# One denominator chain for both scan directions, another bank pair for the second context update, and a reordered first output tile and end, in a diffusion block

## Chip, cores and metric

The kernel runs on one core of one Trainium2 chip. The metric is device time in microseconds (us), lower is better. The engines are PE (TensorE, the matrix products), DVE (VectorE), ACT (ScalarE), POOL (GpSimd) and SP (SyncE, which issues most transfers). Each runs its own instructions in order and waits for the others on semaphores.

## What is computed

One layer of a hybrid backbone on 1024 latent and 256 context tokens of 1024 channels, in float32: a normalisation, a token mixer with two branches (a bidirectional chunkwise mLSTM and a gated MLP), an output projection, a SwiGLU feed-forward and a final normalisation. The change lies in the mLSTM scan, in the output projection and at the final normalisation. The scan, cut to what matters (one direction of one head, chunks of 128 tokens):

```python
def step(carry, inp):
    C, n, m = carry
    ...
    num = s @ v + w_prev[..., None] * (q @ C)
    den = sum(s, axis=-1) + w_prev * (q @ n)
    h = num / max(abs(den), exp(-m_t))[..., None]
    kw = k * w_src[..., None]
    C_new = w_c * C + kw.T @ v
    n_new = w_c * n + sum(kw)
...
out = merged @ w_out
...
xs = xs + g2x * swiglu(...)
return rmsnorm(xs, final_g)
```

## The kernel before

All float32 products of the projections are done in three products of a reduced format: an operand x is split into x_hi (ACT copies it) and x_lo (DVE subtracts), and hi·hi, hi·lo and lo·hi are summed. A stage of weights is one 1 MB block in two halves `raw[0]`, `raw[1]`, split into `whi`, `wlo`; SP loads the next block into a half as soon as DVE has signalled `w_ready` for it.

**The heads.** Four heads run one after the other (head 0 written out, heads 1 and 2 in a loop of PE, head 3 written out), in `head` on PE and `attend` on DVE. After the head's projections the scan runs over ten steps j of one chunk each, two of them context (j = 0, 1), in both directions d at once. In step j PE makes, for each direction, the update product `kw·vaug` (L2274, signal `dc_done`), into bank 2 + d of PM (PSUM has eight banks: PD[0], PD[1] with two each, PM with four). DVE reads the bank and makes the next state from it, `Cst` (L1593, L1597, signal `c_ready`); the next update may overwrite the bank after that. From j = 2 on PE also makes the numerators and the denominator of the latent chunk in one bank: the chunk's own part `work·vaug` (L2291) and the part of the past `WB·Cst` (L2292, signal `num_done`). DVE makes from the denominator's column a small chain of three instructions on 128x1 (`den`, L1611, L1613, L1614), each waiting for the one before (`own.link`), and then scales the 256 numerators into `Hh` (L1617, or L1620 in the second half, signal `h_written`). One 128x256 piece of the `wlo` split of the next head's weights (L1365) is done in each of the steps 2 to 9. On DVE a step therefore stands as: two state updates, one split piece, then chain and scaling of direction 0, then of direction 1. `work` is made ahead of the scan from the scores in banks 0 and 1 of PM (L1583, signal `sw_ready`).

After the scan PE goes on with the next head's projection (`channels`, L2095; in head 3 `v_part`, L2218), which needs the split weights' second half from its fifth of eight k on, while DVE normalises `Hh`; then PE transposes `Hh` (L2307), and DVE multiplies by the output gate (L1632).

**The output projection.** `out_tile(hf, t)` (L2422) makes one tile of 128 tokens x 512 columns: 8 k x 3 products. A tile of 512 columns uses two weight blocks of 256, buffers A and B. Tiles 0 to 3 of the first half are made for k = 0 to 6, then for k = 7; tile 4 waits until DVE has added tile 0 to the residual (`residual`, L1854 and L1857, signal `out_res`). ACT splits block B (L894) only when PE has made the last product of the stage before; DVE follows (L1357).

**The end.** The last stage makes token tiles 0 to 7 of the feed-forward's output (L2527). DVE adds each to the residual (L2018; tile 7 in halves, L2055), ACT sums the squares (L1330, L1333), DVE makes 1/sqrt of the mean by a chain of 12 instructions (`rsqrt`, L1344 to L1350), scales the tile by it and by the gain (`write_out`, L2043), and SP stores it (L697, L701). Tile t - 1 is finished behind the sum of tile t. Tile 6 is finished ahead of and between the sums of the two halves of tile 7.

Of the kernel before, what the change touches and what calls it, by code (L numbers as in the profile page):

```python
# [29 lines left out]
F32 = mybir.dt.float32  # L30
F32R = mybir.dt.float32r
I32 = mybir.dt.int32
ALU = mybir.AluOpType
# [4 lines left out]
P = 128  # L38
D = 1024
# [27 lines left out]
LINKS_H = 74  # L67
# [55 lines left out]
def build(nc, x, c, ctx, c_ctx, w_ada, b_ada, norm1_g, norm2_g, w_in, conv_w, conv_b, gate_b, head_g,  # L123
# [17 lines left out]
    with es:  # L141
# [25 lines left out]
        with ExitStack() as sM:  # L167
# [24 lines left out]
            with ExitStack() as sH:  # L192
# [9 lines left out]
                with ExitStack() as s1:  # L202
# [6 lines left out]
                    den = sb("den", [P, 2, 4], stack=s1)  # L209
# [74 lines left out]
        with ExitStack() as sF:  # L284
# [21 lines left out]
            with ExitStack() as s7:  # L306
                fg = sb("fg", [P, D], stack=s7)
                junkF = sb("junkF", [P, D], stack=s7)
            sa = sb("sa", [P, 2, NLAT], stack=sF)
# [18 lines left out]
        PD = [es.enter_context(nc.psum_tensor(f"PD{s}", [P, 2 * HALF], F32)) for s in range(2)]  # L328
# [58 lines left out]


# [494 lines left out]
        def _(act):  # L883
# [108 lines left out]
            def o_out(h, T, m):  # L992
# [3 lines left out]
                nc.scalar.activation(sgo[:, m, :], PD[m][:, :], ACT.Tanh, scale=0.5).then_inc(slot_free[m], 1)  # L996
                act.wait_ge(slot_free[m], h * 5 + 6)
# [35 lines left out]
            o_out(0, T_H, 0)  # L1033
            weights_b(0)
            weights_d(0)
            o_out(0, T_H, 1)
            split_hi(96, A)
            squares(0)
# [3 lines left out]
            with act.Fori(1, HEADS) as h:  # L1042
# [14 lines left out]
                for m in range(2):  # L1057
                    o_out(h, T, m)
                split_hi(h * 64 + 96, A)
                own.enter(h, LT, 1)  # L1060
# [276 lines left out]
        def _(dve):  # L1337
# [31 lines left out]


# [196 lines left out]
            def attend(h):  # L1567
# [17 lines left out]
                for j in range(TT):  # L1585
                    for d in range(2):
# [3 lines left out]
                        bank = PM[:, (2 + d) * HALF:(2 + d) * HALF + DVA - 1]  # L1590
# [9 lines left out]
                    if j >= 2:  # L1600
                        split_lo_piece(h * 3 + (N_H + 3), A, j - 2)
                    if j < CT:
                        continue
                    for d in range(2):

                        t = tile_of(d, j)
                        at = d * HALF if j % 2 else 0
                        bank = (PM if j % 2 else PD[d])[:, at:at + DV]
                        bden = (PM if j % 2 else PD[d])[:, at + DV:at + DV + 1]
                        dve.wait_ge(num_done, h * 16 + (2 * (j - CT) + d + 1))  # L1610
                        own.link(v.tensor_scalar(den[:, d, 0:1], bden, -1.0, hc[:, 2, d, t:t + 1],  # L1611
                                                 ALU.mult, ALU.max))
                        own.link(v.tensor_tensor(den[:, d, 1:2], bden, den[:, d, 0:1], ALU.max))  # L1613
                        own.link(v.reciprocal(den[:, d, 2:3], den[:, d, 1:2]))  # L1614
# [438 lines left out]
            for e in range(2):  # L2053
# [3 lines left out]
                if e == 0:  # L2057
                    write_out(LT - 2, whole)
# [528 lines left out]
```

## Time and profile before

| | |
|---|---|
| median of 3 runs | 1810.24 us (1808.37 to 1811.42) |
| profiled execution | 1810.4 us |
| its span, first to last instruction | 1808.7 us |
| PE busy | 1760.9 us (97%) |
| DVE, ACT, POOL busy | 1081.5, 602.0, 168.8 us |
| granted TensorE clock, mean | 0.993 of full speed |

The profiled execution took 1.7 us more than its span. "Busy" sums the time in which an engine had an instruction under way; products overlap, so 97% doesn't say that PE could not be faster. Times below are counted from the span's start. L12 is line 12 of the kernel before.

### The profile page before, as it was taken

What the parts mean: (1) busy time and instruction counts of PE and PEld (TensorE: products, weight loads), DVE (VectorE), ACT (ScalarE), POOL (GpSimd) and SP (SyncE); (2) the same over time, 40 slices, a digit from 0 to 9 for tenths busy, and PEclk for the clock granted to TensorE, in tenths of its full rate; (3) what the DMA queues carried; (4) which work ended last, traced back from release to release, by engine and by line L of the source; (5) the groups of instructions that cost most, each with busy time, mean ns of one, the idle gap of its engine ahead of it and who ended that gap; (6) DMA issues with size and microseconds to landing.
All of it is one profiled execution on the core that took longest, in us unless ns stands there. A gap on an engine that the chain in (4) does not pass through costs nothing.

```text
span 1808.7 us, 23195 instructions
## 1 busy us (share of the span) xinstructions
PE 1760.9 (97%) x8556; PEld 1469.8 (81%) x8556; DVE 1081.5 (60%) x1706; ACT 602.0 (33%) x937; POOL 168.8 (9%) x212
## 2 busy tenths in 40 slices
PE   6899999999999999999999999999999999999997
PEld 3697887979788888888888788888888888888886
DVE  4677636575457767546333436865655656566657
ACT  6533241422233324445210213443443333221112
POOL 1002020200212001111100100000000001222210
PEclk9999999999999999999999999999999999999999
DMA  7211110212059123433533343122222232722212
GB/s 305 70 49 35 59 47 24 78 38 71 12 179 319 51 82 100 154 119 132 217 95 98 124 149 128 36 98 89 70 93 70 85 101 70 276 108 93 95 44 94
DMA packets 100131, 187.76 MB, mean 104 GB/s; under 512 B 5810, under 2 KB 74562, under 8 KB 95714
## 3 DMA queue, kind: packets, MB, share of 16 engines
q1 hardware_dynamic: 83906, 130.11, 21.0%
q0 software_dynamic: 16160, 56.77, 8.9%
q8 instruction: 42, 0.69, 0.2%
q14 instruction: 23, 0.19, 0.0%
HBM read 150.11 MB, written 36.75 MB: 103 GB/s over the span
## 4 chain that ended last, share of the span: by engine, by line
PE 89%; DVE 7%; issue 2%; ACT 1%; DMA 0%; DVEq 0%; SPq 0%; ACTq 0%
PE PD L2095 23%; PE PM L2507 11%; PE PD L2507 11%; PE PD L2527 7%; PE PM L2527 6%; PE PD L2422 5%; PE PD L2381 4%; PE PM L2381 4%; PE PD L2205 4%; PE PD L2111 4%; PE PD L2218 1%; PE PM L2441 1%; PE PD L2441 1%; PE PM L2358 1%; PE PD L2180 1%
## 5 line engine op out<-in xcount | busy, mean ns | idle before, releaser
L2095 PE MATMUL PD<-R_hi,whi 128*128 128x512 f32 x480 | 149.3, 392 | 0.0
L2095 PE MATMUL PD<-R_lo,whi 128*128 128x512 f32 x480 | 148.0, 390 | 0.0
L2095 PE MATMUL PD<-R_hi,wlo 128*128 128x512 f32 x480 | 147.8, 389 | 0.0
L867 POOL TENSOR_TENSOR w_raw<-w_raw,g2B 128x2048 f32<-128x2048 f32 x11 | 50.8, 4620 | 652.4 <-DMA w_raw<-in_w_ff 488.4
L2095 PEld LDWEIGHTS PD<-R_lo,whi 128*128 128x128 f32 x480 | 90.1, 188 | 19.0
L2095 PEld LDWEIGHTS PD<-R_hi,wlo 128*128 128x128 f32 x480 | 90.1, 188 | 19.0
L2095 PEld LDWEIGHTS PD<-R_hi,whi 128*128 128x128 f32 x480 | 89.0, 188 | 18.3 <-issue 0.5
L1888 DVE TENSOR_TENSOR ws_lo<-S,ws_hi 128x512 fp32r<-128x512 f32 x76 | 56.3, 742 | 77.2 <-ACT ws_hi L1239 77.2
L894 ACT ACTIVATE whi<-raw 128x1024 fp32r<-128x1024 f32 x56 | 56.2, 1049 | 127.1 <-PE PD L2095 124.5
L2111 PE MATMUL PD<-whi,R_hi 128*128 128x256 f32 x256 | 72.7, 284 | 0.8 <-ACT vaug L960 0.8
L2111 PE MATMUL PD<-wlo,R_hi 128*128 128x256 f32 x256 | 72.4, 283 | 0.0
L2111 PE MATMUL PD<-whi,R_lo 128*128 128x256 f32 x256 | 72.4, 283 | 0.0
L2018 DVE TENSOR_TENSOR xs<-PM,xs 128x1024 f32<-128x1024 f32 x39 | 47.6, 1222 | 34.6 <-PE PM L2527 34.6
L2018 DVE TENSOR_TENSOR xs<-PD,xs 128x1024 f32<-128x1024 f32 x40 | 48.2, 1221 | 32.5 <-PE PD L2527 32.5
L1357 DVE TENSOR_TENSOR wlo<-raw,whi 128x1024 fp32r<-128x1024 f32 x48 | 56.6, 1219 | 6.8 <-ACT whi L894 6.8
L1239 ACT ACTIVATE ws_hi<-S 128x512 fp32r<-128x512 f32 x76 | 47.5, 625 | 31.8 <-DVE S L1902 17.4
L1239 ACT ACTIVATE ws_hi<-rawF 128x512 fp32r<-128x512 f32 x60 | 37.6, 629 | 57.8 <-PE PD L2507 30.4
L2527 PE MATMUL PM<-R_lo 128*128 128x512 f32 x240 | 56.5, 389 | 0.0
L2527 PE MATMUL PD<-R_lo 128*128 128x512 f32 x240 | 56.2, 389 | 0.0
L2527 PEld LDWEIGHTS PD<-R_lo 128*128 128x128 f32 x240 | 45.0, 188 | 9.4
L2527 PEld LDWEIGHTS PM<-R_lo 128*128 128x128 f32 x240 | 45.0, 188 | 9.3
L2527 PE MATMUL PD<-R_hi,f_hi 128*128 128x512 f32 x192 | 51.4, 390 | 0.6 <-issue 0.6
(486 smaller groups left out, 4632.3 us busy)
## 6 DMA issues: line engine op xcount, KB each, us to landing
rawF<-in_w_ff SPq DMA_DIRECT2D x44, 512.0 KB, 4.8
ada<-in_w_ada POOLq DMA_DIRECT2D x32, 512.0 KB, 5.7
raw<-in_w_in SPq DMA_DIRECT2D x30, 512.0 KB, 5.3
f_dram<-Fo SPq DMA_DIRECT2D x11, 1024.0 KB, 4.8
w_raw<-in_w_ff SPq DMA_DIRECT2D x11, 1024.0 KB, 4.9
f_raw<-f_dram SPq DMA_DIRECT2D x11, 1024.0 KB, 6.8
ada_raw<-in_w_ada SPq DMA_DIRECT2D x8, 1024.0 KB, 18.9
rawG<-in_w_in SPq DMA_DIRECT2D x16, 512.0 KB, 4.9
```

The lines of the kernel that those rows point to most:

```text
L894: nc.scalar.activation(whi[buf][:, half * 4 * CW:(half + 1) * 4 * CW], raw[half][:, :], ACT.Copy).then_inc(hi_done, 1)
L1239: nc.scalar.activation(ws_hi[n][:, :, :], left_source(buf, n, sums), ACT.Copy).then_inc(left_hi_d, 1)
L1357: v.tensor_tensor(wlo[buf][:, at], raw[half][:, :], whi[buf][:, at].bitcast(F32), ALU.subtract).then_inc(w_ready[half], 1)
L1888: v.tensor_tensor(ws_lo[n][:, :, :], source, ws_hi[n][:, :, :].bitcast(F32), ALU.subtract)\
L2018: v.tensor_tensor(xs2[:, t, :], wide[t % 4], xs2[:, t, :], ALU.add).then_inc(summed, 1)
L2095: i = mm(dst[:, e * HALF:e * HALF + width], wk[:, k, :], part, start=(k == 0 and step == 0), stop=(k == KT - 1 and step == 2))
L2111: i = mm(PD[s][:, e * HALF:e * HALF + CW], src[:, k, at], wk[:, k, :], start=(k == 0 and step == 0), stop=(k == KT - 1 and step == 2))
L2205: last = mm(dst, src[:, k, t * P:(t + 1) * P], wk[:, k, :, :], start=(k == 0 and step == 0), stop=(k == KT - 1 and step == 2))
L2381: last = mm(held[par][BANK_OF[n]], lt[:, k, :], rt[:, k, :], start=(OPENS[n] and k == 0 and step == 0), stop=(CLOSES[n] and k == KH - 1 an ...
L2422: last = mm(dst, src[:, k, t * P:(t + 1) * P], wk[:, k, :, :], start=(k == 0 and step == 0), stop=(k == KT - 1 and step == 2))
L2507: last = mm(into, lt[:, k, :], moving, start=(OPENS[n] and k == 0 and step == 0), stop=(CLOSES[n] and k == KH - 1 and step == 2), skip_gro ...
L2527: return mm(wide[t % 4][:, e * HALF:(e + 1) * HALF], src[:, k, at], wk[:, k, e * HALF:(e + 1) * HALF], start=(opens and n == 0), stop=(clo ...
```

## The change

Five edits.

1. In the scan one `den` chain on 128x2 serves both directions: it waits for the numerators of both, and the two scalings follow without a wait between them. The banks of PD become one tensor so that a strided access reaches both columns.
2. The split of the next weights: pieces 0 to 3 stay in the scan (steps 2 to 5), the second half is one 128x1024 instruction behind the scan.
3. The second context update (j = 1) goes to banks 0 and 1 of PM, so it waits for `sw_ready` and no longer for the first state. In step 2 the two `own_chunk` products stand ahead of the two `past` products; `sw_ready` and `qw_ready` are waited for apart.
4. ACT does the second part of the output gate (`o_gain`) for half 1 behind the split of the next weights.
5. The first output tile is made in two parts of 256 columns, the first from block A alone. At the end the two halves of tile 7 are summed first; one `rsqrt` on 128x2 serves tiles 6 and 7; tile 6 is scaled and stored behind it. The first half of tile 7 is multiplied by the gain ahead of it.

```diff
-        PD = [es.enter_context(nc.psum_tensor(f"PD{s}", [P, 2 * HALF], F32)) for s in range(2)]
+        PDs = es.enter_context(nc.psum_tensor("PD", [P, 4 * HALF], F32))
+        PD = [PDs[:, s * 2 * HALF:(s + 1) * 2 * HALF] for s in range(2)]
...
+        def update_bank(j, d):
+            bank = d if j == 1 else 2 + d
+            return PM[:, bank * HALF:bank * HALF + DVA - 1]
...
             o_out(0, T_H, 1)
             split_hi(96, A)
+            o_gain(0, 1)
             squares(0)
...
-                        bank = PM[:, (2 + d) * HALF:(2 + d) * HALF + DVA - 1]
+                        bank = update_bank(j, d)
...
-                    if j >= 2:
-                        split_lo_piece(h * 3 + (N_H + 3), A, j - 2)
                     if j < CT:
                         continue
-                    for d in range(2):
-                        t = tile_of(d, j)
-                        at = d * HALF if j % 2 else 0
-                        bank = (PM if j % 2 else PD[d])[:, at:at + DV]
-                        bden = (PM if j % 2 else PD[d])[:, at + DV:at + DV + 1]
-                        dve.wait_ge(num_done, h * 16 + (2 * (j - CT) + d + 1))
-                        own.link(v.tensor_scalar(den[:, d, 0:1], bden, -1.0, hc[:, 2, d, t:t + 1],
-                                                 ALU.mult, ALU.max))
-                        own.link(v.tensor_tensor(den[:, d, 1:2], bden, den[:, d, 0:1], ALU.max))
-                        own.link(v.reciprocal(den[:, d, 2:3], den[:, d, 1:2]))
...
+                    if j < CT + 4:
+                        split_lo_piece(h * 3 + (N_H + 3), A, j - CT)
+                    t0, t1 = tile_of(0, j), tile_of(1, j)
+                    floor = hc[:, 2, :, :].rearrange("p d t -> p (d t)")[:, t0:TT + t1 + 1:TT + t1 - t0]
+                    bden = PM[:, DV:DV + HALF + 1:HALF] if j % 2 else PDs[:, DV:DV + 2 * HALF + 1:2 * HALF]
+                    dve.wait_ge(num_done, h * 16 + (2 * (j - CT) + 2))
+                    own.link(v.scalar_tensor_tensor(out=den[:, 0, :], in0=bden, scalar=-1.0, in1=floor,
+                                                    op0=ALU.mult, op1=ALU.max))
+                    own.link(v.tensor_tensor(den[:, 1, :], bden, den[:, 0, :], ALU.max))
+                    own.link(v.reciprocal(den[:, 2, :], den[:, 1, :]))
+                    for d, t in ((0, t0), (1, t1)):
...
+                split_lo_half(h * 3 + (N_H + 3), A, 1)
                 dve.wait_ge(act_own, h * LT + (TT + 1 + LT))
...
-            norm_factor(LT - 2, LT - 1)
-            for e in range(2):
-                dve.wait_ge(down_done, (NFB - 2) * LT + (LT + 1 + e))
-                v.tensor_tensor(xs2[:, LT - 1, parts[e]], wide[(LT - 1) % 4][:, parts[e]], xs2[:, LT - 1, parts[e]],
-                                ALU.add).then_inc(summed, 1)
-                if e == 0:
-                    write_out(LT - 2, whole)
...
+            add_last(0)
+            add_last(1)
+            weigh_last(0)
             dve.wait_ge(act_own, TT + 1 + HEADS * LT + 2 * LT + LT + 1)
             own.link(v.tensor_tensor(rs[:, 0, LT - 1:LT], rs[:, 0, LT - 1:LT], rs[:, 0, LT:LT + 1], ALU.add))
-            norm_factor(LT - 1, LT + 1)
-            for e in range(2):
-                write_out(LT - 1, parts[e])
+            rsqrt(LT, D, LT - 2)
+            write_out(LT - 2, whole)
+            v.tensor_scalar(xs2[:, LT - 1, parts[0]], ylast[:, parts[0]], rs[:, 2, LT - 1:LT], None, ALU.mult)\
+                .then_inc(o_ready, 1)
+            write_out(LT - 1, parts[1])
...
-                        if j >= 1:
+                        if j == 1:
+                            pe.wait_ge(sw_ready, h * 2 + 2)
+                        elif j == 2:
+                            pe.wait_ge(c_ready, h * 18 + (d + 1))
+                        elif j > 2:
                             pe.wait_ge(c_ready, h * 18 + (2 * j + d - 1))
...
+            def out_part(b):
+                w = [q[:, b, :].rearrange("p (k n) -> p k n", k=KT) for q in (whi2, wlo2)]
+                for k in range(KT - 1):
+                    if k % 4 == 0:
+                        ready(N_O + b, k // 4)
+                    pe.wait_ge(m_ready, k + 1)
+                    for step, (src, wk) in enumerate(((R_hi, w[0]), (R_hi, w[1]), (R_lo, w[0]))):
+                        mm(held[0][0][:, b * CW:(b + 1) * CW], src[:, k, 0:P], wk[:, k, :],
+                           start=(b == 0 and k == 0 and step == 0), stop=False, skip_group_check=True)
...
-            for t in range(2):
-                out_tile(0, t, range(KT - 1))
+            for b in range(2):
+                out_part(b)
+            out_tile(0, 1, range(KT - 1))
```

What moves in the order of instructions is shown at three places; an L number is a line of the kernel that the piece is from, the change's lines lie some 30 further down.

DVE, one full step of the scan in head 0, before: the state updates, a split piece, then chain and scaling twice.

```order
L1597 SCALAR_TENSOR_TENSOR Cst<-Cst,hc,PM 128x257 x2
L1365 TENSOR_TENSOR wlo<-raw,whi 128x256
L1611 TENSOR_SCALAR den<-PM,hc 128x1
L1613 TENSOR_TENSOR den<-PM,den 128x1
L1614 RECIPROCAL den<-den 128x1
L1617 TENSOR_SCALAR Hh<-PM,den 128x256
L1611 TENSOR_SCALAR den<-PM,hc 128x1
L1613 TENSOR_TENSOR den<-PM,den 128x1
L1614 RECIPROCAL den<-den 128x1
L1617 TENSOR_SCALAR Hh<-PM,den 128x256
```

The same step in the change: three small instructions in place of six, and the two scalings together.

```order
L1618 SCALAR_TENSOR_TENSOR Cst<-Cst,hc,PM 128x257 x2
L1379 TENSOR_TENSOR wlo<-raw,whi 128x256
L1630 SCALAR_TENSOR_TENSOR den<-PM,hc 128x2
L1632 TENSOR_TENSOR den<-PM,den 128x2
L1633 RECIPROCAL den<-den 128x2
L1637 TENSOR_SCALAR Hh<-PM,den 128x256 x2
```

PE, the start of the scan in head 0 with what each product waits for, before.

```order
L2274 MATMUL PM<-vaug,kw 128x257 [waits slot_free0,slot_free1,kw_ready,ktok_ready]
L2274 MATMUL PM<-vaug,kw 128x257
L2274 MATMUL PM<-vaug,kw 128x257 [waits c_ready] x4
L2291 MATMUL PD<-vaug,work 128x257 [waits c_ready,slot_free0,qw_ready,sw_ready]
L2292 MATMUL PD<-Cst,WB 128x257
L2291 MATMUL PD<-vaug,work 128x257 [waits slot_free1,c_ready]
L2292 MATMUL PD<-Cst,WB 128x257
```

The same in the change: the second update waits for `sw_ready` alone, the third for the first states, and step 2's own parts no longer wait for a state.

```order
L2309 MATMUL PM<-vaug,kw 128x257 [waits slot_free0,slot_free1,kw_ready,ktok_ready]
L2309 MATMUL PM<-vaug,kw 128x257
L2309 MATMUL PM<-vaug,kw 128x257 [waits sw_ready] x2
L2309 MATMUL PM<-vaug,kw 128x257 [waits c_ready] x2
L2318 MATMUL PD<-vaug,work 128x257 [waits slot_free0]
L2318 MATMUL PD<-vaug,work 128x257 [waits slot_free1]
L2322 MATMUL PD<-Cst,WB 128x257 [waits c_ready,qw_ready]
L2322 MATMUL PD<-Cst,WB 128x257 [waits c_ready]
```

DVE, the end, before: the last instruction of tile 6's chain, then the first half of tile 7, tile 6's scaling, the second half, and tile 7's chain.

```order
L1350 SCALAR_TENSOR_TENSOR rs<-rs 128x1
L2055 TENSOR_TENSOR xs<-PM,xs 128x512
L2043 SCALAR_TENSOR_TENSOR xs<-xs,rs,fg 128x1024
L2055 TENSOR_TENSOR xs<-PM,xs 128x512
L2060 TENSOR_TENSOR rs<-rs 128x1
L1344 TENSOR_SCALAR rs<-rs 128x1
```

The same place in the change: tile 5's scaling, both halves of tile 7, the product with the gain, and one chain for both tiles; tile 6's scaling stands behind that chain.

```order
L2064 SCALAR_TENSOR_TENSOR xs<-xs,rs,fg 128x1024
L2077 TENSOR_TENSOR xs<-PM,xs 128x512 x2
L2083 TENSOR_TENSOR ylast<-xs,fg 128x512
L2089 TENSOR_TENSOR rs<-rs 128x1
L1358 TENSOR_SCALAR rs<-rs 128x2
```

## Rows read from the trace of the kernel before

**Rows 1.** The page, part 1: busy time, share of the span, instructions.

```profile
PE 1760.9 (97%) x8556; PEld 1469.8 (81%) x8556; DVE 1081.5 (60%) x1706; ACT 602.0 (33%) x937; POOL 168.8 (9%) x212
```

**Rows 2.** What PE waited for: us in total, times, longest us.

```profile
PE PM L2274 <- DVE Cst L1597: 3.9, 12, 0.3
...
PE PD L2422 <- DVE wlo L1357: 2.6, 1, 2.6
...
PE PM L2274 <- DVE Cst L1593: 1.9, 1, 1.9
...
PE PM L2441 <- DVE R_lo L1881: 1.1, 1, 1.1
```

**Rows 3.** Timeline, DVE, one step of head 1: start, duration, instruction.

```profile
276.07 0.86 DVE L1597 SCALAR_TENSOR_TENSOR Cst<-Cst,hc,PM 128x257 f32<-128x257 f32 x2
276.85 0.42 DVE L1365 TENSOR_TENSOR wlo<-raw,whi 128x256 fp32r<-128x256 f32 x1
277.19 0.21 DVE L1611 TENSOR_SCALAR den<-PD,hc 128x1 f32<-128x1 f32 x1
...
277.83 0.48 DVE L1617 TENSOR_SCALAR Hh<-PD,den 128x256 f32<-128x256 f32 x1
278.23 0.21 DVE L1611 TENSOR_SCALAR den<-PD,hc 128x1 f32<-128x1 f32 x1
...
279.26 0.86 DVE L1597 SCALAR_TENSOR_TENSOR Cst<-Cst,hc,PM 128x257 f32<-128x257 f32 x2
```

**Rows 4.** Timeline, PE, scan of head 1 (x4 are two float32 products).

```profile
266.11 3.53 PE L2274 MATMUL PM<-vaug,kw 128*128 128x257 f32 x12
...
271.21 1.03 PE L2274 MATMUL PM<-vaug,kw 128*128 128x257 f32 x4
...
273.81 1.03 PE L2274 MATMUL PM<-vaug,kw 128*128 128x257 f32 x4
...
291.21 0.72 PE L2095 MATMUL PD<-R_hi,whi 128*128 128x512 f32 x2
```

**Rows 5.** Timeline, head 0: the scores' weighting, and PE's start behind the scan.

```profile
157.57 2.36 DVE L1583 TENSOR_TENSOR work<-PM,work 128x1024 f32<-128x1024 f32 x2 [5.73 <-PE PM L2257]
...
185.59 0.73 PE L2095 MATMUL PD<-R_hi,whi 128*128 128x512 f32 x2
```

**Rows 6.** Busy by stretch: us, PE, PEld, DVE, ACT, POOL, granted clock, DMA share, GB/s.

```profile
161.00:165.00 4.00, 3.85 (x11) 2.80 (x10) 2.22 (x5) 0.00 (x0) 1.25 (x3) 0.57 0.63 206
...
1035.00:1039.00 4.00, 3.62 (x9) 2.92 (x10) 3.63 (x4) 0.30 (x1) 2.76 (x6) 0.57 0.97 299
...
1142.00:1146.00 4.00, 3.41 (x15) 2.87 (x16) 2.50 (x4) 2.46 (x5) 0.00 (x0) 1.00 0.31 108
```

**Rows 7.** Timeline, PE, head 3: start of the scan.

```profile
477.32 3.53 PE L2274 MATMUL PM<-vaug,kw 128*128 128x257 f32 x12
```

**Rows 8.** Chain that ended last, head 3: PE behind the scan.

```profile
503.14 11.77 PE PD L2218 x96
```

**Rows 9.** Chain that ended last, output projection.

```profile
1035.38 77.99 PE PD L2422 x336
```

**Rows 10.** Timeline, output projection: last of block 2's split, PE's tile 4.

```profile
1053.62 1.22 DVE L1357 TENSOR_TENSOR wo_lo<-raw,wo_hi 128x1024 fp32r<-128x1024 f32 x1 [4.92 <-ACT wo_hi L894]
...
1058.81 0.39 PE L2422 MATMUL PD<-whi,R_hi 128*128 128x512 f32 x1
```

**Rows 11.** Timeline, the end.

```profile
1797.06 0.39 PE L2527 MATMUL PM<-R_hi,f_lo 128*128 128x512 f32 x1
...
1799.61 1.28 DVE L2043 SCALAR_TENSOR_TENSOR xs<-xs,rs,fg 128x1024 f32<-128x1024 f32 x1
1800.81 0.68 DVE L2055 TENSOR_TENSOR xs<-PM,xs 128x512 f32<-128x512 f32 x1
...
1804.85 1.42 DVE L2043 SCALAR_TENSOR_TENSOR xs<-xs,rs,fg 128x512 f32<-128x512 f32 x2
```

**Rows 12.** Transfers of the last 10 us: issues, KB each, median us to landing.

```profile
out_x<-xs SPq DMA_DIRECT2D x1, 512.0 KB, 2.6
out_x<-xs SPq DMA_DIRECT2D x2, 256.0 KB, 2.0
```

**Rows 13.** Timeline, DVE: output gate of head 0.

```profile
209.43 2.36 DVE L1632 TENSOR_TENSOR sgo<-PM,sgo 128x1024 f32<-128x1024 f32 x2 [12.38 <-PE PM L2307]
```

More of the change, by code:

```diff
@@ L208, in build @@
                     hgh = sb("hgh", [P, 2], stack=s1)
-                    den = sb("den", [P, 2, 4], stack=s1)
+                    den = sb("den", [P, 4, 2], stack=s1)
                     work = sb("work", [P, 2, NLAT + 2 * PAD], stack=s1)
@@ L1056, in _ @@
                 weights_d(h)
-                for m in range(2):
-                    o_out(h, T, m)
+                o_out(h, T, 0)
+                o_gain(h, 0)
+                o_out(h, T, 1)
                 split_hi(h * 64 + 96, A)
+                o_gain(h, 1)
                 own.enter(h, LT, 1)
@@ L1368, in split_lo_piece, with split_lo_half @@
                     i.then_inc(w_ready[half], 1)
+            def split_lo_half(n, buf, half):
+                at = slice(half * 4 * CW, (half + 1) * 4 * CW)
+                dve.wait_ge(hi_done, n * 2 + (half + 1))
+                v.tensor_tensor(wlo[buf][:, at], raw[half][:, :], whi[buf][:, at].bitcast(F32), ALU.subtract)\
+                    .then_inc(w_ready[half], 1)
             for first, end in ((0, 4), (4, 7), (7, TT)):
@@ L2277, in head, with own_chunk @@
                         continue
-                    if j == CT:
-                        pe.wait_ge(sw_ready, h * 2 + 2)
-                        pe.wait_ge(qw_ready, h * 2 + 2)
-                    for d in range(2):
-                        t = tile_of(d, j)
-                        lat = (t - CT) * L
-                        at = d * HALF if j % 2 else 0
-                        bank = (PM if j % 2 else PD[d])[:, at:at + DVA - 1]
-                        pe.wait_ge(c_ready, h * 18 + (2 * j + d - 1))
+                    def own_chunk(d, bank, lat, t):
                         if j == CT:
@@ L2291, in head, with past @@
                         mm(bank, work[:, d, PAD + lat:PAD + lat + L], vaug[:, t, 0:DVA - 1], start=True, stop=False)
+                    def past(d, bank, lat):
+                        pe.wait_ge(c_ready, h * 18 + (2 * j + d - 1))
                         mm(bank, WB[:, d, lat:lat + L], Cst[:, d, j % 2, 0:DVA - 1], start=False, stop=True)\
                             .then_inc(num_done, 1)
+                    tiles = [tile_of(d, j) for d in range(2)]
+                    lats = [(t - CT) * L for t in tiles]
+                    banks = [PM[:, d * HALF:d * HALF + DVA - 1] if j % 2 else PD[d][:, 0:DVA - 1] for d in range(2)]
+                    if j == CT:
+                        for d in range(2):
+                            own_chunk(d, banks[d], lats[d], tiles[d])
+                        pe.wait_ge(qw_ready, h * 2 + 2)
+                        for d in range(2):
+                            past(d, banks[d], lats[d])
+                    else:
+                        for d in range(2):
+                            own_chunk(d, banks[d], lats[d], tiles[d])
+                            past(d, banks[d], lats[d])
                 if not last:
```

27 lines of the change are left out of this document (19 added, 8 removed).

## The prediction

> **What bounds the kernel now.** I read the page's busy line first: PE is busy 97% of the span [rows 1], so most of the time can't be touched by an edit of waits, and an edit is worth what PE idles, or spends at half clock, in the stretch it touches. PE's waits name such places [rows 2]: 3.9 us before update products that wait for `Cst`, 1.9 us once at the first state of head 0, 2.6 us once for `wlo` at the output projection. Then come the stages themselves, on the timelines of DVE and PE.
>
> In the scan DVE sets the pace. One step of head 1 lasts 279.26 - 276.07 = 3.19 us [rows 3]: two states 0.78 (276.07 to 276.85), the split piece 0.34, a chain of three small instructions 0.64 (277.19 to 277.83), a scaling 0.40 (277.83 to 278.23), and chain and scaling once more. PE needs less: where it still runs ahead, six float32 products take 273.81 - 271.21 = 2.60 us, 0.433 each [rows 4]. A scan has 18 update products and 32 for the numerators, 50 x 0.433 = 21.65 us, if PE never waits; head 1 takes 291.21 - 266.11 = 25.10 [rows 4].
>
> All sums are made against the profiled execution, 1810.4 us, 0.16 above the median of the runs. A measurement tells about 0.2%, 3.6 us, from no change.
>
> **Scan, heads 1 and 2.** One chain and four pieces fewer: a step on DVE becomes 0.78 + 0.34 + 0.64 + 2 x 0.40 = 2.56 us in steps 2 to 5, and 2.22 without the piece. Both lie below PE's 2.60, so PE becomes the bound. The chain now waits for both numerators, and the next step's states are queued behind it on DVE; but they lie two steps deep, since PE issues the next updates ahead of the numerators. An instruction on 128x2 isn't in the trace; its chain lies between 0.64, what three 128x1 take, and twice that, what the two chains took. I take 0.64: 128x256, 256 times the data, lasts only 0.48 against 0.21 [rows 3]. The gain is between 0 (chain doubled) and 25.10 - 21.65 = 3.45 a head; I take 3.45, and the same for head 2, which runs the same loop: **6.9 us**. The split's second half goes behind the scan: chain 0.64, two scalings 0.80, then 1.22 as in [rows 10], so it is ready some 2.9 us after PE's last product. The next projection needs it only from its fifth k on, after 24 products x 0.227 = 5.4 us (0.227 from [rows 9], where 77.99 less 1.7 of slow start falls on 336 products). Hidden. What DVE does behind the scan ends later by that 1.22, but before the output gate DVE idles 12.38 us [rows 13]. The ACT edit is costed at nothing: `split_hi` comes earlier by one gating instruction, and the gate is used as late as those same 12.38 us tell; without that cover it would cost that instruction on 128x1024 once a head, 1.2 us by the nearest row [rows 10].
>
> **Head 0.** Here the second update waits for the first state, which stands on DVE behind the weighting of the scores: PE idles 1.9 us [rows 2], and in the stretch behind it the granted clock is 0.57, mostly the lower of its levels, 1.2 GHz [rows 6]. The new wait is for `sw_ready`, the end of that weighting, 157.57 + 2.36 = 159.93 [rows 5]. 48 products from 159.98 on end at 159.98 + 20.78 = 180.76 at full clock, against 185.59 [rows 5]: 4.8 us. PE still idles 1.6 us. Of the idle stretches in the trace, 1.9 and 2.6 us were followed by 0.57, 1.1 us by 1.00 [rows 2, 6]. 1.6 is nearer to 1.9, so I take it that the clock falls again: 0.57 over 4 us means 3.4 us at half rate, 1.7 us lost. The gain is **3.1 us**, with 4.8 and 3.1 as ends.
>
> **Head 3.** The scan would end at 477.32 + 21.65 = 498.97 [rows 7] instead of 503.14 [rows 8]. But behind it stands `v_part`, with products of 256 columns, 11.77 / 96 = 0.123 each [rows 8], which needs the split's second half after only 12 of them, 1.47 us. That half is ready at 498.97 + 0.16 + 0.64 + 0.80 + 1.22 = 501.8 (0.16: 1.03 that the two updates last, less 2 x 0.433 [rows 4]). So the next thing late is that split, and PE stalls 1.4 us. Before, PE stood at the same product at 503.14 + 1.47 = 504.61; now 501.9: **2.7 us**. The clock I take to hold, 1.4 being nearer to 1.1 than to 1.9.
>
> **Output projection.** Before, PE idles from 1032.78 to 1035.38 for the split of block B, and then runs at 0.57 [rows 2, 6, 9]. In the change the first part reads block A alone, 21 products of 256 columns x 2 parts: 42 x 0.123 = 5.2 us, to 1038.0. The rest ahead of tile 4 is tiles 1 to 3 (63 products of 512 columns) and k = 7 of all four (12): 75 x 0.227 = 17.0, to 1055.0. Tile 4 then waits for tile 0's residual, which DVE makes behind the split that ends at 1053.62 + 1.22 = 1054.84 [rows 10], a split of a block that DMA brings in. Two additions on 128x512, 0.68 each as in [rows 11], and 0.1 of handing over: PE starts tile 4 at 1056.3, not 1058.81 [rows 10]. **2.5 us**; the bounds are 4.0, if the split moves forward too, and 1.5, if it comes later. A new idle of 1.3 us appears; the clock I take to hold, by 1.1.
>
> **End.** PE's last product ends at 1797.45 [rows 11]. Now both halves of tile 7 are summed then, and not tile 6 finished first: the second sum starts at 1797.5 instead of 1800.81, and the chain behind it, 1804.85 - 1800.81 = 4.04 [rows 11], ends at 1801.5. What is scaled behind the chain grows by tile 6: 1.20 (1799.61 to 1800.81), then half of tile 7 by a plain product, some 0.4 to 0.7, then the other half, about 0.7. DVE ends at 1803.9 instead of 1806.27, 2.4 earlier. But 512 KB of tile 6 are now stored in front of tile 7's halves: it is issued at 1802.8 and takes 2.6 us, and a further 256 KB adds 2.6 - 2.0 = 0.6 [rows 12]: 1802.8 + 2.6 + 2 x 0.6 = 1806.6, against 1806.3 + 2.0 = 1808.3. **1.65 us**. The ends: 2.4 if the stores don't hinder each other, and 1.2 if the last, issued at 1803.9, takes 2.6 + 0.6. The Trainium skill ("DMA: Bandwidth & Descriptors", "Anatomy of one DMA — SWDGE (gpsimd) path") fits a transfer of that path as about 2.0 us plus bytes at 436 GB/s; 1 MB would be 4.4 us by it, and the gain 1.1. Rows of this kernel's SP queue, 2.6 us for 512 KB, where that fit gives 3.2, speak against it.
>
> **Sum.** 3.1 + 6.9 + 2.7 + 2.5 + 1.65 = 16.85; 1810.4 - 16.85 = **1793.6 us**.
>
> **The rivals.**
>
> (a) The clock. It holds in head 0 too: 1.7 more, 1791.9. Or it falls also behind one or both of the new idles of head 3 and of the output projection: 1795.3 or 1797.0. For and against are the four stalls above; no row lies between 1.1 and 1.9. The Trainium skill ("TensorE: Matmul & The Clock Gate") says that an idle engine goes back to the lower rate, which [rows 6] show too; by that alone every new idle would cost, 1797.0.
>
> (b) DVE stays the bound in the scan. If two neighbours don't overlap, states and scalings take 0.48 each [rows 3], and a step with a piece 0.96 + 0.42 + 0.64 + 0.96 = 2.98: 0.38 over PE in four steps of four heads, 6 us, about 1799; with a chain of twice the length 3.20 and 2.86, and the scan's 12.7 us are all but lost: 1806. Against: two states start 0.39 apart, though one lasts 0.48 [rows 3]. The Trainium skill ("VectorE: DVE Perf Modes", "The DRAIN you can't avoid") says that the next operation doesn't start until the pipe is empty; that gives the 2.98. The rows' 0.39 against 0.48 disagrees for neighbours without a wait.
>
> (c) What the scans gain is waited for behind them, by DVE's late normalising or by weights that arrive no sooner: 16.85 less 12.7 leaves 1806.2. Against: 12.38 us of slack [rows 13].
>
> (d) Slower: the joint wait closes the loop over DVE and PE within each step. If PE's next products could start only when the scalings are done, a step would be PE's 2.60, 0.2 to hand over, DVE's 0.64 + 0.80 and states 0.78, 0.1 back: 5.1 us. 1.9 more than 3.19 in 28 of the 32 steps is 53, less the 4 gained elsewhere: 1859. It decides from a step of over 3.34 us on, where 28 x 0.15 eats those 4. Against: update j + 1 needs only the state made ahead of the chain, and numerators alternate between two bank pairs, so the loop of 5 us spans two steps, 2.5 each.
>
> (e) The idle of PE moves to places that I don't see, and nothing is left: 1810.
>
> **How the numbers follow.** Forecast 0.40; (a) 0.25 for the clock holding, 0.15 for falling more often; (b) 0.08, (c) 0.05, (d) 0.03, (e) 0.04. The range takes in the forecast and (a), with the open ends of output projection and end: low 1789.6 (1791.9 less 1.5 and 0.75, rounded), high 1797.5; (b) to (e), 0.2, are outside. Faster by over 0.2% are all but (d) and (e): 0.93; same 0.04, slower 0.03.
>
> **What would show it.** DVE's timeline: three `den` instructions a step, steps of 2.60 us set by PE, and no waits of update products for `Cst` behind step 2. If steps of 2.9 with a piece show up, it is (b); if PE waits for `Hh`, (d). Head 0: PE resumes at about 160.0, and its granted clock in the next 4 us tells the forecast from (a). Head 3: a wait of 1.4 us for `wlo` in the middle of the first `v_part`. Output projection: PE goes on at once on block A, no wait for block B, but about 1.3 us for `xs` at tile 4. The end: the last DVE instruction 2.4 us closer to PE's last product, the last store less so. I would be wrong above all if the steps of the scan stayed near 3.2, since 9 of the 17 us hang on them.

## The result and the profile after

The changed kernel took 1794.76 us (median of 4 runs, 1793.51 to 1796.54), the kernel before, beside it, 1810.1: a ratio of 0.9917, 95% interval 0.9899 to 0.9934, or 15.3 us less. Four more runs of the changed kernel later gave 1793.78, ratio 0.9907 (0.9891 to 0.9922). The forecast was 1793.6, range 1789.6 to 1797.5. The profiled execution took 1793.51, with a span of 1791.8 us against 1808.7.

The page, part 1, of the kernel after (before: [rows 1]): PE is busy 9.3 us less in a span that is 16.9 us shorter.

```profile
PE 1751.6 (98%) x8577; PEld 1471.9 (82%) x8577; DVE 1062.6 (59%) x1587; ACT 602.0 (34%) x937; POOL 169.2 (9%) x212
```

What PE waited for (us in total, times, longest), the kernel after. The waits for `Cst` of [rows 2] are gone. In their place stand three that the prediction named: for the residual at tile 4, for `work` in head 0, for the second half of the split in head 3.

```profile
PE PD L2466 <- DVE xs L1878: 2.4, 1, 2.4
...
PE PM L2309 <- DVE work L1604: 1.6, 1, 1.6
...
PE PD L2249 <- DVE wlo L1388: 1.2, 1, 1.2
```

**The scan's step** (before: [rows 3]). DVE's timeline of the kernel after, in head 0, shows one step with a split piece, and the beginning of a step without one.

```profile
170.40 0.87 DVE L1618 SCALAR_TENSOR_TENSOR Cst<-Cst,hc,PM 128x257 f32<-128x257 f32 x2
171.18 0.42 DVE L1379 TENSOR_TENSOR wlo<-raw,whi 128x256 fp32r<-128x256 f32 x1
171.62 0.16 DVE L1630 SCALAR_TENSOR_TENSOR den<-PM,hc 128x2 f32<-128x2 f32 x1
171.81 0.16 DVE L1632 TENSOR_TENSOR den<-PM,den 128x2 f32<-128x2 f32 x1
172.00 0.17 DVE L1633 RECIPROCAL den<-den 128x2 f32<-128x2 f32 x1
172.20 0.88 DVE L1637 TENSOR_SCALAR Hh<-PM,den 128x256 f32<-128x256 f32 x2
173.00 0.87 DVE L1618 SCALAR_TENSOR_TENSOR Cst<-Cst,hc,PM 128x257 f32<-128x257 f32 x2
174.22 0.16 DVE L1630 SCALAR_TENSOR_TENSOR den<-PD,hc 128x2 f32<-128x2 f32 x1 [0.35 <-PE PD L2322]
```

The step is 173.00 - 170.40 = 2.60 us. The chain on 128x2 takes 172.20 - 171.62 = 0.58, a little less than 0.64 for one on 128x1. Without a piece DVE idles 0.35 and waits for PE; with one it is just below PE: by these rows and the piece's 0.34 of [rows 3] its own work is 0.78 + 0.34 + 0.58 + 0.80 = 2.50. PE's timeline of head 1 after (before: [rows 4]) shows the other side: updates every 2.60 us, no wait, and a scan of 282.87 - 261.39 = 21.48 us.

```profile
261.39 2.77 PE L2309 MATMUL PM<-vaug,kw 128*128 128x257 f32 x12
...
268.33 1.03 PE L2309 MATMUL PM<-vaug,kw 128*128 128x257 f32 x4
...
270.93 1.03 PE L2309 MATMUL PM<-vaug,kw 128*128 128x257 f32 x4
...
282.87 0.82 PE L2126 MATMUL PD<-R_hi,whi 128*128 128x512 f32 x2
```

**Head 0** (before: [rows 5]), PE's timeline after: an idle of 1.58 us, and the projection behind the scan at 180.76.

```profile
160.04 2.00 PE L2309 MATMUL PM<-vaug,kw 128*128 128x257 f32 x8 [1.58 <-DVE work L1604]
...
180.76 0.81 PE L2126 MATMUL PD<-R_hi,whi 128*128 128x512 f32 x2
```

Busy times by stretch after, the last columns being granted clock, DMA share and GB/s (before: [rows 6]). The clock stays at 1.00, its upper level of 2.4 GHz, behind the idle of head 0 and behind that of tile 4.

```profile
161.00:165.00 4.00, 4.00 (x20) 3.48 (x19) 2.98 (x10) 0.00 (x0) 1.32 (x3) 1.00 0.61 209
1043.00:1047.00 4.00, 3.86 (x17) 3.21 (x18) 3.35 (x5) 1.06 (x1) 0.00 (x0) 1.00 0.37 129
```

**Head 3** (before: [rows 7, 8]), PE's timeline after: `v_part` begins at 487.41, and its 13th product waits for the split behind the scan.

```profile
487.41 0.38 PE L2249 MATMUL PD<-whi,R_hi 128*128 128x256 f32 x1
...
490.27 0.39 PE L2249 MATMUL PD<-whi,R_hi 128*128 128x256 f32 x1 [1.17 <-DVE wlo L1388]
```

**Output projection** (before: [rows 9, 10]). DVE's timeline after: the second split of block 2 waits for ACT, and the residual (L1875, L1878) stands behind it.

```profile
1040.52 1.23 DVE L1371 TENSOR_TENSOR wo_lo<-raw,wo_hi 128x1024 fp32r<-128x1024 f32 x1 [5.59 <-ACT wo_hi L901]
1041.67 0.69 DVE L1875 TENSOR_TENSOR PD<-PD,xn 128x512 f32<-128x512 f32 x1
1042.39 0.69 DVE L1878 TENSOR_TENSOR xs<-PD,xs 128x512 f32<-128x512 f32 x1
```

On ACT the same view names the transfer, and on PE tile 4, which waits 2.45 us for that residual.

```profile
1039.43 2.15 ACT L901 ACTIVATE wo_hi<-raw 128x1024 fp32r<-128x1024 f32 x2 [5.76 <-DMA raw<-in_w_out]
...
1043.14 0.50 PE L2466 MATMUL PD<-whi,R_hi 128*128 128x512 f32 x1 [2.45 <-DVE xs L1878]
```

**The end** (before: [rows 11, 12]), DVE's timeline after, and under it the transfers of the last 10 us (issues, KB each, median us to landing): a chain for two tiles, three scalings behind it, and stores that take 2.9 us instead of 2.0.

```profile
1781.13 1.48 DVE L2077 TENSOR_TENSOR xs<-PM,xs 128x512 f32<-128x512 f32 x2
...
1786.10 1.28 DVE L2064 SCALAR_TENSOR_TENSOR xs<-xs,rs,fg 128x1024 f32<-128x1024 f32 x1
1787.30 0.48 DVE L2092 TENSOR_SCALAR xs<-ylast,rs 128x512 f32<-128x512 f32 x1
1787.70 0.75 DVE L2064 SCALAR_TENSOR_TENSOR xs<-xs,rs,fg 128x512 f32<-128x512 f32 x1
```

```profile
out_x<-xs SPq DMA_DIRECT2D x1, 512.0 KB, 2.6
out_x<-xs SPq DMA_DIRECT2D x2, 256.0 KB, 2.9
```

**All profiles by stretch.** Starts differ between executions (the first update of head 0 came at 157.4 to 160.5 us), so effects of one or two us are read from stretches. The clock is part of the reason: the three profiles with a start of 160.5 (two chains, old end, tile 6 in halves) have a fall at 134 us, ahead of head 0. This is that stretch with two chains; the kernel after shows 1.00 in the same window.

```profile
134.00:138.00 4.00, 4.00 (x12) 3.03 (x11) 2.89 (x13) 0.59 (x3) 0.00 (x0) 0.59 0.40 112
```

The columns of the table: "head n" runs from the scan's first update to the first product behind it, for head 3 to the 13th product of `v_part`; "projection" from the end of the issue of PE's last product before the output projection to the start of DVE's sum for token tile 6; "end" from there to the end of the span, which is given to 0.1 us, so that column is good to 0.05. An f marks a stretch in which the granted clock was lowered.

| kernel | median us | head 0 | head 1 | head 2 | head 3 | projection | end |
|---|---|---|---|---|---|---|---|
| before | 1810.1 | 28.23 f | 25.10 | 24.88 | 27.35 | 759.44 f | 16.65 |
| after | 1794.76 | 23.33 | 21.48 | 21.49 | 24.52 | 758.16 | 15.32 |
| after, again | 1793.78 | 23.33 | 21.49 | 21.49 | 24.53 | 758.33 | 15.28 |
| two chains | 1804.71 | 25.28 | 23.64 | 23.49 | 27.66 | 759.92 f | 15.29 |
| eight pieces | 1794.16 | 23.32 | 21.48 | 21.49 | 23.20 | 759.96 f | 15.35 |
| old banks | 1799.39 | 25.75 f | 22.25 | 22.25 | 25.30 | 759.79 f | 15.30 |
| before + edit 1 | 1801.14 | 25.76 f | 22.25 | 22.25 | 23.96 | 759.44 f | 16.64 |
| whole tile | 1796.09 | 23.33 | 21.49 | 21.48 | 24.53 | 757.84 | 15.35 |
| residual first | 1791.52 | 23.33 | 21.48 | 21.48 | 24.53 | 755.46 | 15.29 |
| old end | 1795.18 | 23.33 | 21.48 | 21.48 | 24.53 | 758.27 | 16.64 |
| tile 6 in halves | 1796.07 | 23.33 | 21.48 | 21.48 | 24.53 | 758.25 | 14.89 |
| gain first | 1795.38 | 23.33 | 21.48 | 21.49 | 24.53 | 757.13 | 15.37 |
| scores early | 1795.56 | 21.49 | 21.49 | 21.48 | 24.52 | 759.93 f | 15.28 |
| all four | 1788.64 | 21.48 | 21.48 | 21.48 | 23.20 | 755.46 | 14.87 |

### The profile page after: what moved, and what is told of

The parts are those of the page before. It is cut to its first block, busy times and chain, and to the rows that moved or that the text cites. A ratio compares the mean times of both kernels' runs of the same rounds, so it can differ in the third digit from the quotient of the medians.

```text
span 1791.8 us, 22991 instructions
## 1 busy us (share of the span) xinstructions
PE 1751.6 (98%) x8577; PEld 1471.9 (82%) x8577; DVE 1062.6 (59%) x1587; ACT 602.0 (34%) x937; POOL 169.2 (9%) x212
## 4 chain that ended last, share of the span: by engine, by line
PE 92%; DVE 4%; ACT 1%; DMA 1%; issue 1%; DVEq 0%; SPq 0%; ACTq 0%
PE PD L2126 23%; PE PM L2564 11%; PE PD L2564 11%; PE PD L2584 7%; PE PM L2584 6%; PE PD L2425 4%; PE PM L2425 4%; PE PD L2466 4%; PE PD L2236 4%; PE PD L2142 4%; PE PM L2309 2%; PE PM L2497 1%; PE PD L2249 1%; PE PD L2497 1%; PE PM L2402 1%
```

## The experiments

The theory: DVE's small instructions set the scan's step, the one chain took it below PE's; the banks save waits at the start of a scan; the first output tile in parts only moves an idle; the end gives 0.9 of its 2.25 us back to transfers. Each edit was undone or done alone.

**Two chains** (edit 1 undone).

```diff
-                    dve.wait_ge(num_done, h * 16 + (2 * (j - CT) + 2))
...
+                    for d in range(2):
...
+                        dve.wait_ge(num_done, h * 16 + (2 * (j - CT) + d + 1))
+                        own.link(v.tensor_scalar(den[:, d, 0:1], bden, -1.0, hc[:, 2, d, t:t + 1],
+                                                 ALU.mult, ALU.max))
+                        own.link(v.tensor_tensor(den[:, d, 1:2], bden, den[:, d, 0:1], ALU.max))
+                        own.link(v.reciprocal(den[:, d, 2:3], den[:, d, 1:2]))
...
```

> The changed kernel with edit 1 undone: two denominator chains a step, four split pieces, new banks. Theory (DVE's instructions set the step of the scan, and the one chain took it below PE's 2.60 us): steps of 3.19 us with a piece and 2.85 without, 4 x 0.59 + 4 x 0.25 = 3.4 us a head lost, about 1807 us. Rival (the other banks of the second update, which let PE run ahead, brought the scans' gain): steps stay at 2.60, about 1795.

Measured: 1804.71 us, ratio 0.997 (0.9959 to 0.998). The theory's step came, but the loss is 2.0 to 2.2 us in heads 0 to 2 and 3.1 in head 3, not 3.4 in each. PE's updates in head 0 show why:

```profile
166.69 1.03 PE L2311 MATMUL PM<-vaug,kw 128*128 128x257 f32 x4
169.29 1.03 PE L2311 MATMUL PM<-vaug,kw 128*128 128x257 f32 x4
172.25 1.13 PE L2311 MATMUL PM<-vaug,kw 128*128 128x257 f32 x4 [0.20 <-DVE Cst L1618]
175.44 1.13 PE L2311 MATMUL PM<-vaug,kw 128*128 128x257 f32 x4 [0.32 <-DVE Cst L1618]
178.63 1.13 PE L2311 MATMUL PM<-vaug,kw 128*128 128x257 f32 x4 [0.33 <-DVE Cst L1618]
181.49 1.13 PE L2311 MATMUL PM<-vaug,kw 128*128 128x257 f32 x4
```

The spacings are 2.60, 2.96, 3.19, 3.19 and 2.86. PE is ahead at the start, and pays only when that lead is used up; my 3.4 counted the first two steps as lost already. It also counted the last ones, though PE needs no further state behind its last update (the last row): heads 0 to 2 lose only 0.1 to 0.2 us there. In head 3 PE also waits 0.7 us for `Hh` at the first product behind the scan and 1.5 instead of 1.2 at the 13th. The rival is out: with the new banks alone the steps are not 2.60. The other edits without this one bring 0.3% of the 0.8%.

**Eight pieces** (edit 2 undone).

```diff
-                    if j < CT + 4:
+                    if j >= CT:
                         split_lo_piece(h * 3 + (N_H + 3), A, j - CT)
...
-                split_lo_half(h * 3 + (N_H + 3), A, 1)
```

> The changed kernel with edit 2 undone: a split piece in each of the steps 2 to 9, nothing of it behind the scan. Theory (a step with a piece takes DVE 2.56 us, still under PE's 2.60): scans as long as in the changed kernel, 21.5 us, and the stall of 1.17 us in the first v_part of head 3 is gone, about 1793.6. Rival (fewer pieces are part of what took DVE below PE): steps 6 to 9 get 0.1 to 0.3 us longer, 2 to 5 us in four heads, 1796 to 1799.

Measured: 1794.16 us, ratio 0.9908 (0.9889 to 0.9926). Scans of 21.48 us as before, and head 3's stretch is 24.52 - 23.20 = 1.32 us shorter, without the wait for `wlo`. So with one chain the pieces fit in the scan, and moving them costs 1.3 us in head 3 and gains nothing. The median doesn't resolve that (in its profile the clock fell at tile 4).

**Old banks** (edit 3 undone).

```diff
-            bank = d if j == 1 else 2 + d
+            bank = 2 + d
...
-                        if j == 1:
-                            pe.wait_ge(sw_ready, h * 2 + 2)
...
+                        if j >= 1:
                             pe.wait_ge(c_ready, h * 18 + (2 * j + d - 1))
...
```

> The changed kernel with edit 3 undone: the second update in the bank of the first, waiting for the first state, old order in step 2. Theory (one chain alone brings the steps to 2.60; the banks save only the waits at the start of a scan): heads 1 to 3 get 0.8 us longer each at the start, head 0 about 0.7 and, if the idle of 1.9 us is again followed by half clock, 1.7 more: 1797.9 to 1799.6. Rival (the loss at the start is caught up later in the scan): 1795.

Measured: 1799.39 us, ratio 0.9935 (0.9917 to 0.9954). Heads 1 to 3 are 0.77 us longer each, head 0 is 25.75 - 23.33 = 2.42. PE's timeline and its stretch in head 0 show the old idle and the lowered clock:

```profile
160.66 3.32 PE L2305 MATMUL PM<-vaug,kw 128*128 128x257 f32 x8 [1.91 <-DVE Cst L1614]
```

```profile
161.00:165.00 4.00, 3.85 (x11) 2.84 (x10) 2.21 (x5) 0.00 (x0) 1.60 (x3) 0.63 0.44 180
```

**Edit 1 alone**, on the kernel before; the scalings then use `den[:, 2, d:d + 1]`.

```diff
-                        dve.wait_ge(num_done, h * 16 + (2 * (j - CT) + d + 1))
...
+                    dve.wait_ge(num_done, h * 16 + (2 * (j - CT) + 2))
+                    own.link(v.scalar_tensor_tensor(out=den[:, 0, :], in0=bden, scalar=-1.0, in1=floor,
+                                                    op0=ALU.mult, op1=ALU.max))
...
```

> The kernel before with edit 1 alone. Theory: steps of 2.60 us in all four scans, with all eight pieces in them; heads 1 and 2 gain 2.8 each, head 3 3.6 (no split behind the scan), head 0 2.4 to 4.1 by its clock: 11.6 to 13.3 us, 1797 to 1798.5. Rival (edits 1 to 3 only work together): less than 6 us, over 1804.

Measured: 1801.14 us (1798.42 to 1802.31), ratio 0.9946 (0.9924 to 0.9967). By stretch 2.47 + 2.85 + 2.63 + 3.39 = 11.3 us, under the expected 11.6 to 13.3; the median says 9.8 and lies above the expected times, in runs 3.9 us apart. Steps are 2.60 in all scans, so the rival is out: edit 1 is most of the gain and needs none of the others.

**Whole tile** (edit 5, first output tile, undone; a wait, on `m_ready`, goes by k again and isn't shown).

```diff
-            for b in range(2):
-                out_part(b)
-            out_tile(0, 1, range(KT - 1))
+            for t in range(2):
+                out_tile(0, t, range(KT - 1))
```

> The changed kernel with the first output tile made whole again. Theory (the part made early only moves PE's idle time to tile 4, which waits for a residual behind a split behind a transfer, and that idle is mostly followed by half clock as the old one was): from the last product of the stage before to the sum of token tile 6 takes 759.4 us as in the kernel before, against 758.2 in the profile of the changed kernel and 759.8 to 760.0 in three of the runs above, where the clock fell: about 1794.8, no change that can be measured. Rival (2.5 us gained as the prediction has it): 1797.3.

Measured: 1796.09 us, ratio 0.9924 (0.9907 to 0.9942), which overlaps the changed kernel's; its four runs are two near 1794.5 and two near 1797.7. In the profile the old idle of 2.6 us was not followed by a fall:

```profile
1022.00:1026.00 4.00, 3.53 (x16) 2.97 (x17) 3.71 (x4) 0.22 (x1) 2.85 (x6) 1.00 0.96 296
```

At equal clock the part gains nothing: 757.84 whole against 758.16 to 758.33 in four profiles with the part and its full idle; with a fall, 759.44 against 759.79 to 759.96. The whole tile is 0.3 to 0.5 us better in both, if anything. A likely cause, not tried alone, is arithmetic: 42 products of 256 columns at 0.123 take 5.2 us, 21 of 512 at 0.227 only 4.8. Theory's 759.4 missed for the lack of a fall; that the idle only moves holds.

**Residual first.** On DVE the residuals of tiles 0 and 1 stand ahead of the split that held them up.

```diff
-            split_lo(N_O + 2, 2)
+            split_lo(N_O + 2, 2, (0,))
             residual(0, 0)
             residual(0, 1)
+            split_lo(N_O + 2, 2, (1,))
```

> The changed kernel with the residuals of tiles 0 and 1 ahead of the second half of the split that they stood behind on DVE. Theory (that split, late by its transfer, holds the residual up, and nothing else does): the idle of 2.45 us at tile 4 is gone and with it the half clock behind it, 2.4 to 4.2 us less: 1790.6 to 1792.4. Rival (the tokens that the residual adds arrive as late as the weights, or the split is then late for the second half): idle stays or moves, 1794 to 1795.

Measured: 1791.52 us, ratio 0.9895 (0.9879 to 0.9912). DVE now takes the residual as soon as PE has made tile 0:

```profile
1040.02 0.70 DVE L1875 TENSOR_TENSOR PD<-PD,xn 128x512 f32<-128x512 f32 x1 [3.73 <-PE PD L2467]
...
1042.70 2.35 DVE L1371 TENSOR_TENSOR wo_lo<-raw,wo_hi 128x1024 fp32r<-128x1024 f32 x2
```

PE has no wait at tile 4, and the stretch is 755.46: 2.7 us less than without a fall, 4.4 less than with one. So against the kernel before the early part of the first tile and this order are together worth 759.44 - 755.46 = 4.0 us, 2.4 at equal clock (757.84). The part without the order is worth nothing, by the run above; the order without the part was not run.

**Old end** (edit 5, end, undone).

```diff
-            add_last(0)
-            add_last(1)
-            weigh_last(0)
...
+            norm_factor(LT - 2, LT - 1)
+            for e in range(2):
...
+                if e == 0:
+                    write_out(LT - 2, whole)
...
```

> The changed kernel with the end of the kernel before. Theory (the new end gains 2.25 us on DVE and gives back 0.9 by the larger transfers behind it): from the start of tile 6's sum to the end of the span 16.65 us against 15.3, about 1796.1. Rival (DVE's 2.25 us in full): 1797.0.

Measured: 1795.18 us, ratio 0.9915 (0.9898 to 0.9932). The median doesn't tell it; the stretch does: 16.64 against 15.32, so the new end gains 1.3 us.

**Tile 6 in halves**, each with a store of its own (the stores' lines are not shown).

```diff
-            write_out(LT - 2, whole)
+            write_out(LT - 2, parts[0])
+            write_out(LT - 2, parts[1])
```

> The changed kernel with tile 6 scaled and stored in two halves of 256 KB. Theory (the end is bound by 1 MB of transfers that start with the first store): the first store is issued 0.6 us earlier, from tile 6's sum to the end 14.6 to 14.8 us instead of 15.3, about 1794.2. Rival (the end is bound by DVE's last instruction, issue and 2.9 us of a transfer): 15.3 to 15.5, 1794.8 to 1795.

Measured: 1796.07 us, ratio 0.9919 (0.9903 to 0.9936), after a start at 160.5 in the profile instead of 157.4. The end is 14.89 us, 0.4 less than 15.32, a little short of the 0.5 to 0.7 of the theory, but far from the rival's: the transfers bind the end at least in part.

**The changed kernel again, and edit 4 undone** (the gate's part ahead of the split on ACT; the first has no edit).

```diff
             o_out(0, T_H, 1)
+            o_gain(0, 1)
             split_hi(96, A)
-            o_gain(0, 1)
...
```

> The changed kernel once more, for a second profile and a better median. Theory (a new idle of 2.45 us at tile 4 in every run, followed by half clock in some): 1793.5 to 1796.5, the stretch from the last product before the output projection to tile 6's sum 758.2 us without half clock or 759.8 to 760.0 with it; head 0's scan 23.3 at full clock, its idle being 1.6 us in each of eight runs so far without a fall. Rival (head 0's clock held by chance): 25.0 in it.

> The changed kernel with edit 4 undone: the gate's second part on ACT ahead of the split of the next weights. Theory (ACT's order is covered on both sides): no change, scans of 21.5 us in heads 1 and 2 and 23.3 in head 0, time within 1 us of the changed kernel beside it. Rival (the split of the weights comes too late for the first piece in step 2): DVE waits up to 1.2 us in step 2, and PE up to 0.3 to 1 us a head, 1 to 4 us slower.

Measured: 1793.78 and 1795.38 us (1793.52 to 1796.7), ratios 0.9907 (0.9891 to 0.9922) and 0.9915 (0.9902 to 0.9929). The scans are the same to 0.01 us, so edit 4 costs and brings nothing there. With edit 4 undone tile 4's idle was 1.4 us, since the second split of block 2 began 21.2 us behind the stage before, not 22.2 to 22.4 as in the other profiles with the early part and the old order of the residuals. The weights for that split are asked for at the same point in all 14 profiles, 3.7 us behind the stage, among ten transfers of 512 KB that POOL issues; what differs is how long they take, 16.2 to 16.8 us in four profiles (before, edit 1 alone, whole tile, edit 4 undone) and 17.4 to 17.6 in the other ten. Two causes fit in part, and neither is shown. In the ten a 16 KB transfer on the instruction queue (q8) begins 18.7 to 18.9 us behind the stage, ahead of the landing, and in the first three of the four only behind it, at 21.6 to 25.9; but with edit 4 undone it begins at 18.7 too. And edit 4 itself is in all of the ten and in only one of the four, so that it costs 1 us at this place isn't excluded.

**Scores early.**

```diff
-                if first:
-                    channels(1, n + 2, A, 1, R_hi, R_lo, ks=range(KH, KT))
-                else:
+                if not first:
                     free(8)
...
                 i.then_inc(s_done, 1)
-                if not first:
+                if first:
+                    channels(1, n + 2, A, 1, R_hi, R_lo, ks=range(KH, KT))
+                else:
                     free(9)
```

> The changed kernel with head 0's score products ahead of the second half of the projection before the scan, as heads 1 and 2 have it. Theory (what is left of head 0's start is the weighting of the scores, which begins only when PE has made them): DVE's weighting begins when ACT's weights are ready, 1.2 us earlier against the scan, PE's idle of 1.6 us shrinks to 0.4, head 0's scan 22.1 us: 1.2 us less. Rival (the weighting then waits for ACT's weights just as long): 23.3 us, no change.

Measured: 1795.56 us, ratio 0.9918 (0.9904 to 0.9932): no gain in the median, and every run is above those of the changed kernel beside it; the profile has a fall at tile 4 and a start at 158.6. By stretch head 0 is 21.49 us, 1.84 less, as long as the others; PE's timeline has no idle in it any more, but a new wait of 0.5 us ahead of the scores. That side counts too: from the product behind PE's idle of 0.92 us, near 98 us, to the scan's first update it takes 60.1 us here and 59.3 in the nine other profiles without a fall at 134 us and without this edit. So 0.8 of the 1.84 is given back, and 1.1 is left, close to the theory's 1.2, by stretches alone.

```profile
158.57 2.77 PE L2309 MATMUL PM<-vaug,kw 128*128 128x257 f32 x12
```

```profile
PE PM L2286 <- DVE ktok L1597: 0.5, 1, 0.5
```

**All four**: eight pieces, residual first, tile 6 in halves, scores early.

> The changed kernel with eight pieces in the scan, the residuals first, tile 6 in halves and the scores early together. Theory (four places of their own, so the gains add): 1.3 in head 3, 2.7 to 4.4 at the output projection, 1.2 in head 0 and 0.4 at the end, 5.6 to 7.3 us less than the changed kernel beside it, 1787.5 to 1789.2. Rival (the gains overlap, since an idle that goes in one place comes back in the next): 1790 to 1792.

Measured: 1788.64 us, ratio 0.9881 (0.9866 to 0.9896), 5.1 us less than the changed kernel beside it, in every run below all of its runs. The median misses the expected 5.6 by 0.5. By stretch the changes add: 1.85 + 1.33 + 2.87 + 0.41 = 6.46 against the changed kernel's second profile. Of this 0.8 goes to the longer way to the scan, which leaves 5.7; the rest of the later start (159.18 against 157.54) lies ahead of 98 us, where no edit is. What PE waits for behind the start is short:

```profile
PE PM L2498 <- DVE R_lo L1901: 1.1, 1, 1.1
PE PD L2585 <- issue: 0.6, 1, 0.6
PE PM L2287 <- DVE ktok L1597: 0.5, 1, 0.5
```

## Why the prediction was right, and where it was not

The time was right, 1793.6 against 1794.76 and 1793.78, and most of its terms; two were wrong, head 0 by 1.8 too little and the output projection by 1.2 too much. That they nearly cancelled is luck, and so is that the two profiled executions began their scans alike, at 157.36 and 157.43 us.

**Heads 1 and 2: right.** Forecast 6.9 us, measured (25.10 - 21.48) + (24.88 - 21.49) = 7.0. The step of 2.60 with PE as the bound, the chain on 128x2 at the price of one on 128x1, and the hidden split all came. Rival (b) fell as its rows said: two scalings last 0.88 together, not twice 0.48. The Trainium skill ("VectorE: DVE Perf Modes", "The DRAIN you can't avoid") has the next operation wait for an empty pipe, but adds that one that isn't held back starts earlier; the prediction left the addition out. The 0.88 of two neighbours without a wait agrees with it. The other half of (b), a chain of twice the length, had a price beforehand: the prediction says that no instruction on 128x2 is in the trace, but the kernel before has some, in `rsqrt`, and they take 0.16 us, like most of those on 128x1 (busy us in total, mean ns of one, idle before):

```profile
L1350 DVE SCALAR_TENSOR_TENSOR rs<-rs 128x2 f32<-128x2 f32 x6 | 1.0, 162 | 0.2
```

Rival (d) didn't show: no wait of PE for `Hh`. That edit 1 carries this, and not the banks, is shown by the runs with two chains and with edit 1 alone.

**Head 0: wrong by 1.8.** Forecast 3.1, measured 28.23 - 23.33 = 4.9. The end of the scan, 180.76, and the idle of 1.6 came as worked out. The step that failed is the clock: I took it to fall behind 1.6 us because that is nearer to 1.9 than to 1.1. It stayed at 1.00 in all nine profiles with that idle. The 4.8 that I had named as the other end was the right value, by case (a).

**Head 3: right.** Forecast 2.7 with a stall of 1.4, measured 27.35 - 24.52 = 2.83 with one of 1.17. I had called the split the next thing late, but not seen that leaving the pieces in the scan was free.

**Output projection: wrong.** Forecast 2.5 with an idle of 1.3 at tile 4, and 1.5 as the lower bound; measured 759.44 - 758.16 = 1.3 with an idle of 2.45, and -0.3 to -0.5 where the clock falls again. Two steps failed. The split that holds the residual began not as early as in [rows 10] but later against the stage: 1040.52 - 1018.33 = 22.2 us after its end, against 1053.62 - 1032.61 = 21.0. And I charged the half clock to the kernel before alone and took it to hold after; behind the new idle it fell in four of eight profiles, and behind the old one not in all three. At equal clock the edit is worth -0.3 to -0.5. The two steps account for this: the 2.5 less the 1.6 that a fall costs and less the 1.2 of the later split is -0.3. So most of the 2.5 was clock, which is luck in both kernels.

**End: right, a little small.** DVE's last instruction comes 14.22 - 11.97 = 2.25 us sooner behind tile 6's sum (forecast 2.4), stores give 0.9 of it back (0.75); 1.33 against 1.65, within the ends given.

**Edit 4: right** in the scans, nothing; whether it plays a part in the later split is open. The sum by stretch is 4.90 + 7.01 + 2.83 + 1.28 + 1.33 = 17.35 of the 16.9 between the spans; the rest is small differences between the stretches.

## What to carry to other kernels

Compare the step of a loop on both engines: here three small instructions fewer let DVE fall just below PE's 2.60 (2.56 by the forecast's sum, 2.50 with the chain as measured), and all further relief of DVE in that loop, such as the moved split, was worth nothing or less. When an idle is removed at one product, follow each engine's order up to the next product that waits: the gain of 2.4 to 4.0 us at the output projection was held back by one instruction of the wrong rank on DVE, and came when two residuals were put ahead of it. Read effects of one or two us from stretches between fixed instructions, since medians here moved by as much with the start and the clock.

## What was not expected of the hardware

Granted clock after an idle of PE, from head 0's scan on, over the 14 profiles: behind 1.6 us it never fell (nine profiles), behind 1.9 us always (three), but behind 2.4 to 2.6 us at tile 4 only in four of eight, and behind the 2.6 us at block B in two of three. A fall shows as 0.50, the level of 1.2 GHz, between the moment PE resumes (1035.3 us for 1035.38 in the kernel before) and 1.8 us later (162.8 for 161.01 with edit 1 alone), and costs 1.6 us (759.44 against 757.84 for the same order). The falls at 134 us came without an idle that the trace shows, behind 22 small products, 20 of them on 128x16 in 2.3 us; the kernel after has the same products and no fall. So the length of the idle alone doesn't decide. The Trainium skill ("TensorE: Matmul & The Clock Gate", Part 1) has an idle engine go back to the lower rate; these rows agree for some idles and not for others of the same length. Here is one of those with a fall, the stretch behind tile 4's idle with eight pieces, to be held against 1.00 in the kernel after:

```profile
1042.00:1046.00 4.00, 3.72 (x10) 2.99 (x11) 3.27 (x5) 1.06 (x1) 0.00 (x0) 0.61 0.41 130
```
